# A two-block transformer on one core: opening by halves of chunks, clock fillers, and three orders changed

## What is computed

```python
c_act = silu(c)
for layer in (0, 1):
    sh_a, sc_a, gt_a, sh_m, sc_m, gt_m = split(c_act @ ada_w[layer] + ada_b[layer], 6)
    h = rms_norm(x, attn_norm[layer]) * (1 + sc_a) + sh_a
    mix = diff_attention(h) if layer == 0 else nsa_attention(h, *shared)
    x = x + gt_a * mix
    h = rms_norm(x, mlp_norm[layer]) * (1 + sc_m) + sh_m
    x = x + gt_m * (square(relu(h @ w1)) @ w2)
    if layer == 0:
        shared = nsa_shared_kv(modulated_norm(x))   # compressed, selected and window keys and values
x = rms_norm(x, final_norm)
h = x + mlstm_layer(x);  h = ple_add(h, p[0])
h = h + dilated_layer(h, shared_kv(h));  h = ple_add(h, p[1])
```

## Time and profile before

| | before |
|---|---|
| median of 3 runs | 2116.03 us (2113.04 to 2121.13) |
| the profiled execution | 2119.31 us |
| its span, first to last instruction | 2117.5 us |
| PE busy | 1979.0 us (93%) |
| DVE busy | 1173.3 us (55%) |
| ACT busy | 847.5 us (40%) |
| mean granted clock of PE | 0.958 |
| share of PE in the chain that ended last | 82% |

### The profile page before, as it was taken

One profiled execution on the slowest core, in us unless ns is written; L12 is line 12 of the kernel. 1 busy time (PEld: TensorE's weight loads), 2 busy tenths in 40 slices (PEclk: granted clock), 3 DMA queues, 4 the chain that ended last, 5 costly groups with the idle time before them and its releaser, 6 DMA issues.

```text
span 2117.5 us, 24340 instructions
## 1 busy us (share of the span) xinstructions
PE 1979.0 (93%) x9300; PEld 1632.0 (77%) x9300; DVE 1173.3 (55%) x2049; ACT 847.5 (40%) x1319; POOL 0.2 (0%) x4
## 2 busy tenths in 40 slices
PE   1999989999998999889989999999999999999999
PEld 0877667888886887789977888888787877777877
DVE  8557846665657465556545333435663455755554
ACT  3226723232223533356633231323444444657343
POOL 0000000000000000000000000000000000000000
PEclk9999998999999979589999999999999999999999
DMA  9661053546554222000022222222121232232021
GB/s 355 209 208 41 1 198 140 202 177 216 179 198 159 99 80 80 0 1 2 1 85 86 92 90 97 99 99 99 60 100 60 80 125 79 81 120 80 1 90 60
DMA packets 42216, 223.85 MB, mean 106 GB/s; under 512 B 4444, under 2 KB 5212, under 8 KB 23694
## 3 DMA queue, kind: packets, MB, share of 16 engines
q1 hardware_dynamic: 41602, 222.25, 29.5%
q10 hardware_dynamic: 524, 0.41, 0.1%
HBM read 219.45 MB, written 3.19 MB: 105 GB/s over the span
## 4 chain that ended last, share of the span: by engine, by line
PE 82%; DVE 8%; DMA 4%; ACT 4%; issue 2%; SPq 0%; DVEq 0%; ACTq 0%
PE bank L422 22%; PE bank L423 22%; PE bank L424 22%; PE bank L1564 3%; PE bank L1535 2%; DMA raw<-wts_d 2%; PE bank L1525 1%; DMA adab<-ada_d 1%; ACT wH L403 1%; PE bank L1526 1%; PE bank L2736 1%; DVE wL L408 1%; DMA ada<-ada_d 1%; DVE tmp L532 1%; PE bank L741 1%
## 5 line engine op out<-in xcount | busy, mean ns | idle before, releaser
L422 PE MATMUL bank<-hH,wH 128*128 128x512 f32 x1328 | 530.2, 399 | 59.5 <-DVE hL L541 37.0
L423 PE MATMUL bank<-hL,wH 128*128 128x512 f32 x1328 | 524.8, 395 | 0.0
L424 PE MATMUL bank<-hH,wL 128*128 128x512 f32 x1328 | 524.2, 395 | 0.0
L422 PEld LDWEIGHTS bank<-hH,wH 128*128 128x128 f32 x1328 | 254.7, 192 | 120.8 <-issue 59.3
L1006 ACT ACTIVATE wH<-raw 128x2048 fp32r<-128x2048 f32 x64 | 122.7, 1917 | 468.8 <-PE bank L424 468.8
L408 DVE TENSOR_TENSOR wL<-raw,wH 128x2048 fp32r<-128x2048 f32 x76 | 174.0, 2290 | 228.0 <-ACT wH L403 227.7
L423 PEld LDWEIGHTS bank<-hL,wH 128*128 128x128 f32 x1328 | 254.7, 192 | 53.7 <-issue 1.0
L424 PEld LDWEIGHTS bank<-hH,wL 128*128 128x128 f32 x1328 | 254.2, 191 | 54.1
L1050 DVE TENSOR_TENSOR wL<-raw,wH 128x2048 fp32r<-128x2048 f32 x64 | 146.5, 2289 | 225.8 <-ACT wH L1006 225.8
L403 ACT ACTIVATE wH<-raw 128x2048 fp32r<-128x2048 f32 x76 | 145.3, 1911 | 246.8 <-PE bank L424 208.4
L422 PE MATMUL bank<-aH,wH 128*128 128x512 f32 x512 | 199.2, 389 | 0.0
(11 more groups left out here) (367 smaller groups left out, 2633.4 us busy)
## 6 DMA issues: line engine op xcount, KB each, us to landing
raw<-wts_d SPq DMA_DIRECT2D x140, 1024.0 KB, 4.9
adab<-ada_d SPq DMA_DIRECT2D x96, 512.0 KB, 4.4
ada<-ada_d SPq DMA_DIRECT2D x4, 2048.0 KB, 22.4
bt<-bias_rows SPq DMA_DIRECT2D x1, 4096.0 KB, 13.0
x<-x_d SPq DMA_DIRECT2D x1, 2048.0 KB, 9.8
peF<-ple_d SPq DMA_DIRECT2D x2, 1024.0 KB, 5.6
out_d<-x SPq DMA_DIRECT2D x4, 512.0 KB, 2.7
pF<-p_d SPq DMA_DIRECT2D x2, 512.0 KB, 3.5
```

The source lines that it names most:

```text
L422: pe.matmul(o, l[0], r[0], start=start, stop=False)
L423: pe.matmul(o, l[0], r[1], start=False, stop=False)
L424: return pe.matmul(o, l[1], r[0], start=False, stop=stop)
```

## The change

It joins several edits.

1. **Opening.** The first tiles run by halves of chunks: half 0 (tile 0, chunks 0 to 3), half 1 (tile 1, chunks 0 to 3), then tiles 0 and 1 with chunks 4 to 7; the halves 1 and 2 of `a_in` swap places in the stream. The loads come as columns, c, scale tiles 0 to 3, x, shift tiles 0 to 3, halves 0 and 1, then scale and shift tiles 4 to 7. silu(c) is made with Sigmoid and one product; scale columns are folded in the sum. h is applied in two parts of four chunks. The bias table is loaded behind half 4, when all 16 first sums are made.
2. **Ada slots.** Four slots in place of two, everywhere, and semaphores to match.
3. **Attention's end.** Halves 14 and 15 are loaded ahead of the wait for `y_lo`; the ada tiles 40 to 47 go in fours ahead of halves 16 and 17, the small tables last. The gate and shift columns are closed ahead of `diff_dve`.
4. **first_chunk.** Where a dense stage starts behind a norm, the first chunk's eight matmuls on hH run for all four groups before the four on hL: opening, tile 24, tile 47, both MLPs' first quarter, both ple gates.
5. **Fillers.** `fill` issues n matmuls of ident by ident (128x128 f32) into a bank that is not in use: 13 after three statistics passages, 8 after the two-norm one, 10 in the opening, 3, 5, 6, 9 and 3 in and around the second attention.
6. **Compressed keys.** The evacuation of tile 26 comes before `hi(N_C0 + 1)`, `cmp_pe` waits for two of its banks, and the copy of the second compressed result before `hi(N_B1 + 1)`. `kcH` is held twice so that its score matmuls run over 160 columns; the first block's score matmuls with ksH run over up to 256. What the extra columns write is overwritten or never read.
7. **Values by token** are stored and reloaded two halves later in SP's list.

```diff
-        tiles(i["a_w_in"][0]), tiles(i["a_w_out"][0]), mlp_tiles(i["mlp_w1"][0], i["mlp_w2"][0]),
+    a_in = tiles(i["a_w_in"][0])[[0, 2, 1, 3, *range(4, 12)]]
+        a_in, tiles(i["a_w_out"][0]), mlp_tiles(i["mlp_w1"][0], i["mlp_w2"][0]),
...
+        def first_chunk(pe, b0, w, count):
+            pe.wait_ge(h_hi, count)
+            for m in range(4):
+                pe.matmul(bank[:, b0 + m, :], w(m)[0], hH[:, 0, :], start=True, stop=False)
+                pe.matmul(bank[:, b0 + m, :], w(m)[1], hH[:, 0, :], start=False, stop=False)
+            pe.wait_ge(h_lo, count)
+            for m in range(4):
+                pe.matmul(bank[:, b0 + m, :], w(m)[0], hL[:, 0, :], start=False, stop=False)
...
+                ahead = a in (24, 47) and j == 0
+                if ahead:
+                    first_chunk(pe, 4 * (a % 2), lambda m: wpart(n0 % 2, 0, m * P, P), hbase + 1)
...
+        def fill(pe, o, n):
+            for _ in range(n):
+                pe.matmul(o[:, 0:P], ident[:, :], ident[:, :], start=True, stop=True)
...
+            if s in (1, 2, 3):
+                fill(pe, bank[:, 4 * (next_a % 2) + 3, :], 13)
...
+        def ada_slot(j):
+            return sb["adab"][:, j % 4, :] if j % 4 < 3 else sb["adac"][:, :]
...
         def ada_load(sp, k):
             j = k - ADA_FIRST
-            if j >= 2:
-                sp.wait_ge(ada_used, j - 1)
-            sp.dma_start(sb["adab"][:, j % 2, :], d["ada"][k]).then_inc(ada_in[j % 2], 16)
+            if j < 4:
+                sp.wait_ge(ada_in[j], 16)
+            else:
+                sp.wait_ge(ada_used, j - 3)
+            sp.dma_start(ada_slot(j), d["ada"][k]).then_inc(ada_in[j % 4], 16)
...
         def sp_first(sp):
+            sp.dma_start(cols[:, :], d["cols"]).then_inc(cols_in, 16)
             sp.dma_start(sb["cb"][:, :], d["c"].to_broadcast([P, D])).then_inc(cb_back, 16)
...
+            for e in range(2):
+                for t in (1, 0):
+                    sp.dma_start(sb[f"ada{t}"][:, 4 * e:4 * e + 4, :],
+                                 d["ada"][8 * t + 4 * e:8 * t + 4 * e + 4].rearrange("k p n -> p k n"))\
+                        .then_inc(ada_in[2 * e + 1 - t], 16)
+                    if (e, t) == (0, 1):
+                        sp.dma_start(x[:, :, :], d["x"]).then_inc(x_in, 16)
+                    if (e, t) == (0, 0):
+                        load_half(sp, 0)
+                        load_half(sp, 1)
+            load_half(sp, 2)
...
             for n in range(12):
-                load_half(sp, n + 2)
+                if n >= 1:
+                    load_half(sp, n + 2)
                 for k in range(max(3 * n - 1, 0), min(3 * n + 2, 24)):
                     ada_load(sp, 16 + k)
+                if n == 2:
+                    sp.wait_ge(f_out, 16)
+                    sp.wait_ge(ada_pre, 16)
+                    sp.dma_start(sb["bt"][:, :, :], skewed).then_inc(bt_in, 16)
+            load_half(sp, 14)
+            load_half(sp, 15)
             sp.wait_ge(c_saved, 16)
             sp.wait_ge(y_lo, 8)
             sp.dma_start(sb["cb"][:, :], csave.to_broadcast([P, D])).then_inc(cb_back, 16)
+            for n in (16, 17):
+                for k in range(4):
+                    ada_load(sp, 40 + 4 * (n - 16) + k)
+                load_half(sp, n)
...
+            for e in range(2):
+                for t in (1, 0):
+                    if (e, t) == (0, 0):
+                        sq_dve(dve, 0, range(1, 7))
+                    dve.wait_ge(ada_in[2 * e + 1 - t], 16)
+                    for c in range(4 * e, 4 * e + 4):
+                        a = sb[f"ada{t}"][:, c, :]
+                        gain, first = (col("attn_norm", c), start[:, c:c + 1]) if t else (1.0, col("ada_b", c))
+                        dve.tensor_tensor_reduce(a, a, cb, gain, first, ALU.mult, ALU.add, mod(8 * t + c))\
+                            .then_inc(ada_pre, 1)
+                lo(dve, 2 * e)
+                dve.wait_ge(ada_pre, 8 * e + 8)
+                apply_dve(dve, 0, 0, lambda c: mod(8 + c), lambda c: mod(c), chunks=range(4 * e, 4 * e + 4))
+                if e == 0:
+                    lo(dve, 1)
...
-            for a in range(4):
-                tile_mm(pe, a, 2 * a, hbase=0 if a == 0 else None)
+            pe.wait_ge(w_hi, 1)
+            fill(pe, bank[:, 3, :], 10)
+            for n, (a, j) in enumerate(((0, 0), (1, 0), (0, 1), (1, 1))):
...
-                pe.wait_ge(acc_free[0], 4 * 14)
+                pe.wait_ge(acc_free[0], 4 * 13 + 2)
...
+                    more = min(part.stop + P, T) if i == 0 else part.stop
+                    pe.matmul(bank[:, u % 2, part.start:more], q_stack(4 * g + r, i),
+                              ksH[:, b, g, 0:more - part.start], start=True, stop=False)
...
+                    fill(pe, bank[:, 0, :], 5)
+                    pe.wait_ge(kc_ev, 1)
...
-            act.activation(sb["kcH"][:, :], bank[:, 4, 0:P], ACT.Copy).then_inc(kc_hi, 1)
+            for r in range(2):
+                act.activation(sb["kcH"][:, r, :], bank[:, 4, 0:P], ACT.Copy).then_inc(kc_hi, 1)
...
-                if n == N_K2 + 6:
+                if n == N_K2 + 8:
```

More of the change, by code:

```diff
@@ L228, in place @@
     s("one", [P, 4])
-    t("ada0", [P, 8, D], "h")
+    t("ada0", [P, 8, D], "bias")
     t("ada1", [P, 8, D], "hid")
-    t("adab", [P, 2, D], "ada")
-    t("cb", [P, D], "ada", 8 * K)
+    t("adab", [P, 3, D], "ada")
+    t("adac", [P, D], "misc")
+    t("cb", [P, D], "ada", 12 * K)
     t("ce", [P, D], "misc")
@@ L269, in place @@
     t("vblk", [P, GRP, 4 * HD], "misc", 8320)
-    t("kcH", [P, P], "misc", 12416, F32R)
+    t("kcH", [P, 2, P], "ada", 16 * K, F32R)
     s("kcL", [P, P], F32R)
@@ L453, in tile_mm @@
                     continue
-                for kk in range(4):
+                ahead = a in (24, 47) and j == 0
+                if ahead:
+                    first_chunk(pe, 4 * (a % 2), lambda m: wpart(n0 % 2, 0, m * P, P), hbase + 1)
+                for kk in range(1 if ahead else 0, 4):
                     if hbase is not None:
@@ L614, in stats_two_pe @@
             pe.matmul(both, mean, sq_slot2(7), start=False, stop=True).then_inc(stat_mm, 1)
+            fill(pe, bank[:, 7, :], 8)
         def root_act(act, s, bank_, dst, eps):
@@ L989, in mlp_pe @@
                             continue
-                        for kk in range(4):
+                        if (q, j) == (0, 0):
+                            first_chunk(pe, 4 * st, lambda m: wpart(n0 % 2, 0, m * P, P), hbase - KC + 1)
+                        for kk in range(1 if (q, j) == (0, 0) else 0, 4):
                             k = 4 * j + kk
@@ L1214, in act_first @@
             act.wait_ge(cb_back, 16)
-            act.activation(sb["ce"][:, :], sb["cb"][:, :], ACT.Exp, scale=-1.0).then_inc(first_e, 1)
+            act.activation(sb["ce"][:, :], sb["cb"][:, :], ACT.Sigmoid).then_inc(first_e, 1)
+            act.preload_act_table_set(EXP_LN)
             sq_act(act, 0, xw_loaded, range(KC))
             rstd_act(act, 0, 0)
+            hi(act, 0)
+            act.wait_ge(ada_pre, 8)
+            apply_act(act, 0, lambda c: mod(c), chunks=range(0, 4))
+            hi(act, 1)
             for r in range(2):
@@ L1329, in pe_first @@
             stats_pe(pe, 0, 0)
-            pe.wait_ge(ready, 5)
-            pe.wait_ge(par_in, 80)
+            pe.wait_ge(par_in, 64)
             pe.matmul(bank[0:HEADS, 6, :], sb["rb"][:, :], sb["oh"][:, 0:T], start=True, stop=True).then_inc(f_mm, 1)
             pe.matmul(bank[0:HEADS, 7, 0:P], sb["rb"][:, :], sb["oh"][:, T:640], start=True, stop=True).then_inc(f_mm, 1)
-            for a in range(4):
-                tile_mm(pe, a, 2 * a, hbase=0 if a == 0 else None)
+            pe.wait_ge(w_hi, 1)
+            fill(pe, bank[:, 3, :], 10)
+            for n, (a, j) in enumerate(((0, 0), (1, 0), (0, 1), (1, 1))):
+                if n == 1:
+                    pe.wait_ge(f_row, 2)
+                pe.wait_ge(w_lo, n + 1)
+                if n == 0:
+                    first_chunk(pe, 0, lambda m: wpart(0, 0, m * P, P), 1)
+                for kk in range(1 if n == 0 else 0, 4):
+                    k = 4 * j + kk
+                    pe.wait_ge(h_lo, k + 1)
+                    for m in range(4):
+                        last = three(pe, bank[:, 4 * a + m, :], wpart(n % 2, kk, m * P, P), (hH[:, k, :], hL[:, k, :]),
+                                     k == 0, k == KC - 1)
+                last.then_inc(half_used, 1)
+            for a in range(2, 4):
+                tile_mm(pe, a, 2 * a)
             diff_pe(pe)
@@ L1401, in gelu_act @@
                                ACT.Copy).then_inc(c_ev, 1)
+            if then:
+                then(act)
             act.wait_ge(c_sq, 4 * s + 4)
@@ L1580, in c_scores @@
                     o, g = bank[:, 6 + hd % 2, (hd // 2) * 32:(hd // 2 + 1) * 32], hd // 4
-                    pe.matmul(o, q_stack(hd, i), sb["kcH"][:, g * 32:(g + 1) * 32], start=True, stop=False)
```

(13 more changed lines are left out.)

133 lines of the change are left out of this document (52 added, 81 removed).

## The result

The changed kernel takes 2047.8 us (median of 3 runs, 2046.2 to 2049.36) against 2116.03: ratio 0.9674, 95% interval 0.9642 to 0.9707. Its profiled execution has a span of 2046.0 us against 2117.5, 71.5 us less. In the ratios, 0.001 is 2.1 us. The forecast was 2040, its range 2024 to 2068.

The account below looks back on a forecast made before the run. The tensor engine, busy 1979.0 of 2117.5 us, was taken as the bound, with gains from its waits, low clock and start. Terms summed to 78 us: 2041 from the profiled 2119.3, 2038 from the median; forecast 2040, range 2024 to 2068.

Parts of the forecast that it names:

- opening and first attention's start: First dense matmul at 33.9 instead of 49.97, start at full clock, small stall; earlier ada sum: 16.6 + 2.2 us.
- attention's end: First attention's end: no waits for wL, shorter passage to the next dense matmul, clock kept: 14 us.
- MLP 0's end: Statistics passage after layer 0's MLP: ada wait gone, first_chunk, shorter gap and clock kept: 6.3 us.
- compressed keys, first gap: Gap of 4.20 us at 757.93 falls to 1.25, but the next link limits the gain to 3.4 us.
- second gap: Gap of 2.52 us at 816.08 loses the 1.9 split, and its dip of 2.5 goes: 4.4 us.
- second attention with its fillers and its tail: Fillers and wider scores hold the clock: 10 us in the first stretch, 3 of later dips, 2.5 at the tail: 15.5.
- layer 1's statistics, two norms, gates, values: Layer 1's passage 2.8, before the second block 3.9, ple gates 2.4, values' store two halves later 6.4 us.
- Rival (a): Clock stays low in the second attention, by the rule on transposes: 13.5 us less gain, 2054; chance 0.17.
- (b): Fillers hold the clock nowhere and overrun the gaps: 35 us worse, 2075; chance 0.12.
- (e): Slower: in the opening, SP's loads wait behind ada tiles and VectorE's sums, repeated over eight halves; chance 0.02.
- (c): Opening bound elsewhere, by late x, half 0 or half 5: start at 40, 2046; chance 0.12.
- (d): Second attention's clock holds from 852 on and all dips there vanish: 2031; chance 0.12.

Follow-up runs that it names:

- e3_x_first: Changed kernel with x loaded ahead of the first four scale tiles and VectorE's adds of squares ahead of the first four sums: 2044.96 us, ratio 0.9638.
- e1_no_fill: Changed kernel with all 83 filler matmuls left out: 2058.13 us, ratio 0.9705.
- e2_no_first: Changed kernel without first_chunk, so every dense stage waits for hL of its first chunk: 2059.28 us, ratio 0.9703.
- e8_gelu: Changed kernel with VectorE's low part of the gelu projection's first half moved ahead of its last quarter of q's low part: 2045.35 us, ratio 0.9665.
- e5_narrow: Changed kernel with the widened score matmuls narrow again, fillers kept: 2047.86 us, ratio 0.9678.
- e9_cmp_old: Changed kernel with ScalarE's compressed-key split ahead of the last evacuation again and PE waiting for all four evacuations of tile 26: 2050.98 us, ratio 0.9676.

## Why the prediction was right, and what it missed

Shifts of the same PE instruction between the profile before and the first profile after, cut between the terms where the shift is level, so that each holds its own dips:

| term | forecast | measured |
|---|---|---|
| opening and first attention's start | 18.8 | 18.2 |
| attention's end | 14 | 13.4 |
| MLP 0's end | 6.3 | 6.2 |
| compressed keys, first gap | 3.4 | 4.4 |
| second gap | 4.4 | 0.5 |
| second attention with its fillers and its tail | 15.5 | 17.0 |
| layer 1's statistics, two norms, gates, values | 15.5 | 11.7 |
| sum | 78 | 71.5 |

**Opening.** Each link up to the first dense matmul came within a microsecond, though the sums with a scale column folded in stand 1.27 us apart and not 1.14. The stall near 56 did not come, and half 5 was 0.48 us late at 89.74, which I had called hidden. `e3_x_first` shows what set the start.

**Attention's end and the statistics passages.** The loads in front of `y_lo` and the four slots do what was said. That the gaps would hold 0.3 us and the clock would stay is in the rows above; `e1_no_fill` prices the clock at 1.6 to 3.0 us in each, `e2_no_first` the first chunk at 1.2 us of gap each.

**The step that failed** is "The gap of 2.52 at 816.08 loses the 1.9 split, and its dip (2.5): 4.4 us". The gap went from 2.52 to 1.83, and the dip stayed in the first profile (2.8 us; it was absent in the second). I had removed ScalarE's split from the chain and not asked what VectorE makes for the same matmul: wL, behind q's low part. `e8_gelu` takes the gap to 0.55 with one line moved. It is the rule that I used at the first gap ("the gain stops at the next link"), not used at the second.

**Second attention.** The first profile gained 7.4 us up to 904, net of 1.6 paid ahead of the first score (1.4 of it for the fillers and the second copy, where the forecast had 0.7 and 0.25), 6.6 from there to the tail, and 2.9 at the tail; the forecast had 10, 3 and 2.5. So the parts were off and made up for each other. In the ten profiles with fillers and wide scores the whole is 11.1 to 19.5 us, the middle of them 13.6; the changed kernel's own two, 17.0 and 19.5, are the highest, so part of the agreement is luck. Without any filler it is 9.9, without the attention's fillers 3.2, with narrow scores 10.0, in one profile each. Rival (a), that the clock stays low there, falls: 0.76 and 0.86 in the two profiles of the changed kernel against 0.55. But `e1_no_fill` has 0.70, so what holds the clock isn't the fillers alone, and a part of the stage stays low: at 833 PE waits 2.60 us for VectorE's oB, and no filler stands there. The Trainium skill (TensorE: Matmul & The Clock Gate, part 4 on PE-mode transpose) says that transposes don't count as busy in the same way. The transposes stayed in all twelve runs, and these separate them neither from narrow matmuls nor from the waits. The trace does show that transposes among other matmuls need not bring the clock down: this row is from the same stage of the changed kernel, with 206 transposes among its matmuls and no idle time above 0.81 us.

```profile
919.00:1014.00 95.00, 93.26 (x748) 88.23 (x748) 54.71 (x173) 61.73 (x112) 0.00 (x0) 1.00 0.01 1
```

What share they have in the dips that stand where PE also waits is open.

**Rivals (b) to (e).** (b) falls: fillers hold the clock at the passages. With no fillers at all the kernel is 10 us slower by the medians (5 to 7 by the ratio) and not 35, so the price of (b) was far too high as well: much of the clock comes back as soon as the long gaps go (45.2 us lost to it there, 74.2 before, 31.6 with the fillers). (c) falls with the start at 34.45, though its 2046 is the time measured. (d) did not come: the fastest execution, 2039.0 us, still has five dips in the second attention (10 us), and stands nearer to the forecast than to 2031. (e) did not come.

**What is in the 6.5 us.** 3.9 are the second gap. 3.8 stand in the last row of the table, whose own terms came as forecast (2.6, 3.7, 2.5 and 6.6 us against 2.8, 3.9, 2.4 and 6.4): new dips at 1533 and 1670 (1.7 each) and a longer one at 1922, in code that the change doesn't touch. 0.6 are the opening, and 0.6 the first attention, where a new dip at 174 (3.4 us) outweighs what two old ones give back. The first gap (1.0) and the second attention (1.5) gave more than forecast. The dips at 174 (at half the size) and 1533 stood again in the second profile, the one at 1670 did not. Why the clock falls there isn't settled.

## What to carry over

When an engine's work is taken out of a wait, list what every other engine still makes for the same instruction: the gain ends at the second of them. Fillers pay in a gap that has a known end ahead of a dense stage (1.6 to 3.0 us each here, with no matmul delayed); starting with the parts that are ready pays about as much (1.2 us a passage). An idle time that shrinks because fillers stand in it is no gain: measure between the real matmuls on both sides. Where the clock's dips wander between executions of one program, price an edit by such distances and by medians of several runs, not by the clock of one profile, and not by a ratio whose other side wanders more than the edit is worth.

## What the runs showed of the hardware

Widening is nearly free. At the high clock, a wide and a narrow matmul cost together what two narrow ones do. First the changed kernel, then `e5_narrow`:

```profile
813.02 0.32 PE L1653 MATMUL bank<-kcH,qs 128*128 128x160 f32 x1
813.18 0.21 PE L1656 MATMUL bank<-kcL,qs 128*128 128x32 f32 x1
813.25 0.32 PE L1653 MATMUL bank<-kcH,qs 128*128 128x160 f32 x1
...
827.84 0.26 PE L1656 MATMUL bank<-kcL,qs 128*128 128x32 f32 x1
...
828.06 0.26 PE L1656 MATMUL bank<-kcL,qs 128*128 128x32 f32 x1
```

From 813.02 to 813.25 a pair of 160 and 32 columns takes 0.23 us, two of 32 columns from 827.84 to 828.06 take 0.22.

The same program ran at either level of the clock (1.2 or 2.4 GHz) through the same 96 matmuls of the compressed keys, behind the same 1.22 us of idling: full in seven profiles, half in four. Behind 4.20 us of idling it was half in the two profiles there are, the kernel before's and that of `e9_cmp_old`.
